# A hybrid decoder layer on eight cores: row statistics by matmul, two queues for the last chunk's copies, and another order of the projection's side work

## What is computed

```python
h = rms_norm(x, norm_mix_g)
z = h @ w_in                       # columns: q 1024 | k 256 | v 256 | u_val 1024 | u_gate 1024
q = rope(rms_norm(q, q_norm_g), pos)
k = rope(rms_norm(k, k_norm_g), pos)
a = attn_prompt(q, k, v, sinks)
u = u_val * jax.nn.sigmoid(u_gate)
c, new_c = causal_dwconv(u, c_buf, conv_w, conv_b)
c = jax.nn.silu(layer_norm(c, conv_ln_g, conv_ln_b))     # over the 1024 channels
x = x + jnp.concatenate([a, c], axis=-1) @ w_out
hm = rms_norm(x, norm_mlp_g)
x = x + jnp.square(jax.nn.relu(hm @ w_up)) @ w_down
```

## Time and profile before

| | us |
|---|---|
| the three times | 1243.03, 1243.94, 1368.0 |
| median shown | 1243.94 |
| profiled execution, its own time | 1243.03 |
| its span on core 4, the slowest | 1241.5 |
| spans of the eight cores | 1235.1 to 1241.5 |
| PE busy | 1191.1 (96%) |
| DVE, ACT, POOL busy | 823.4 (66%), 388.3 (31%), 78.6 (6%) |

### The profile page before, as it was taken

How to read it: one execution, slowest core, us unless ns; L and a number is a source line. 1 busy time by engine, 2 the same in 40 slices (tenths; PEclk the granted TensorE clock), 3 DMA queues, 4 the chain that set the end, 5 groups by cost and what they waited for, 6 DMA issues and landing times.

```text
span 1241.5 us, 26331 instructions; the slowest of 8 cores (1235.1 to 1241.5 us)
## 1 busy us (share of the span) xinstructions
PE 1191.1 (96%) x10375; PEld 943.6 (76%) x10375; DVE 823.4 (66%) x1288; ACT 388.3 (31%) x535; POOL 78.6 (6%) x135
## 2 busy tenths in 40 slices
PE   5859999999989999999999999999999999999998
PEld 3536555555657888888888888888888888888887
DVE  5736866666486967676667676666767666766765
ACT  3536555655144544320004330002332001333000
POOL 2301000000001000000000000000000000000000
PEclk9989999999999999999999999999999999999999
DMA  9995164575949796549966556994444995444795
GB/s 245 217 159 58 20 117 91 106 168 109 241 81 181 199 224 121 90 75 238 241 126 97 90 86 132 259 207 80 92 96 84 250 233 113 95 80 91 178 245 193
DMA packets 56637, 180.27 MB, mean 145 GB/s; under 512 B 20140, under 2 KB 23340, under 8 KB 42540
## 3 DMA queue, kind: packets, MB, share of 16 engines
q0 software_dynamic: 29664, 90.74, 46.5%
q1 hardware_dynamic: 21812, 57.21, 13.8%
q10 hardware_dynamic: 5040, 30.65, 7.4%
HBM read 227.44 MB, written 34.68 MB: 211 GB/s over the span
## 4 chain that ended last, share of the span: by engine, by line
PE 83%; DMA 11%; DVE 3%; ACT 1%; issue 1%; SPq 1%; DVEq 0%; POOL 0%; ACTq 0%; POOLq 0%
PE psum L625 83%; DMA arena<-xt 3%; DVE arena L589 3%; ACT arena L585 1%; DMA x<-arena 1%; DMA arena<-x 1%; DMA arena<-arena 1%; DMA arena<-wdn 1%; DMA arena<-tab 1%; DMA arena<-wup 1%; DMA arena<-wq 1%; SPq L572 1%; DVEq L383 0%; POOL arena L572 0%; ACTq L383 0%
## 5 line engine op out<-in xcount | busy, mean ns | idle before, releaser
L625 PE MATMUL psum<-arena 128*128 128x258 f16 (+10 forms) x10375 | 1191.1, 287 | 47.0 <-DMA arena<-wkv 15.8
L625 PEld LDWEIGHTS psum<-arena 128*128 128x128 bf16 (+3 forms) x10375 | 943.6, 98 | 294.2 <-issue 94.0
L589 DVE TENSOR_TENSOR arena<-arena 128x1024 f16<-128x1024 bf16 (+9 forms) x751 | 504.7, 701 | 198.7 <-ACT arena L585 123.8
L589 DVE TENSOR_TENSOR arena<-psum,arena 128x516 f32<-128x516 f32 (+8 forms) x477 | 329.5, 698 | 202.6 <-PE psum L625 178.3
L585 ACT ACTIVATE arena<-arena 128x512 f32<-128x512 f32 (+10 forms) x266 | 251.6, 959 | 281.8 <-DVE arena L589 231.7
L607 ACT COPY arena<-psum 128x516 f32<-128x516 f32 (+2 forms) x69 | 39.7, 575 | 365.1 <-PE psum L625 353.3
L585 ACT ACTIVATE arena<-psum 128x512 bf16<-128x512 f32 (+8 forms) x140 | 77.0, 579 | 130.3 <-PE psum L625 126.9
L585 ACT ACTIVATE arena<-psum,arena 128x344 f32<-128x344 f32 (+6 forms) x50 | 28.1, 589 | 54.2 <-PE psum L625 50.5
L572 POOL DMA_DIRECT2D arena<-wdn x32 | 17.0, 531 | 386.2 <-PE psum L625 349.0
L572 POOL DMA_DIRECT2D arena<-wup x32 | 17.1, 534 | 374.2 <-PE psum L625 369.0
L602 DVE TENSOR_SCALAR arena<-arena 128x1160 bf16<-128x1160 f32 (+2 forms) x27 | 16.0, 592 | 11.9 <-DMA arena<-xt 10.9
(11 more groups left out here) (10 smaller groups left out, 4.4 us busy)
## 6 DMA issues: line engine op xcount, KB each, us to landing
arena<-wup POOLq DMA_DIRECT2D x32, 1024.0 KB, 9.8
arena<-wdn POOLq DMA_DIRECT2D x32, 1024.0 KB, 12.7
arena<-x ACTq DMA_DIRECT2D x23, 1032.0 KB, 13.2
x<-arena SPq DMA_DIRECT2D x15, 1032.0 KB, 14.8
arena<-xt SPq DMA_DIRECT2D x16, 580.0 KB, 15.7
arena<-arena SPq DMA_DIRECT2D x128, 65.8 KB, 4.9
x<-arena SPq DMA_DIRECT2D x16, 516.0 KB, 10.6
arena<-wu POOLq DMA_DIRECT2D x16, 512.0 KB, 7.5
```

The costliest lines, as they stand in the source:

```text
L589: return P.add(eng, lambda e: e.tensor_tensor(out=out.ap, in0=in0.ap, in1=in1.ap, op=op), reads=[in0, in1], writes=[out], cost=cost(eng, o ...
L625: return P.add("pe", lambda e: e.matmul(out.ap, lhsT.ap, rhs.ap, start=start, stop=stop, skip_group_check=free), reads=[lhsT, rhs], writes ...
```

## The change

Four things change in the stages above.

1. Row statistics per token come from PE: ten float32 matmuls with 128 (last: 4) columns of `SS1` as stationary and one column of ones as moving operand give a column for each V tile in bank 6 (`ptk`), and two `Ln` and two `Exp` make `RTK` of it. The ten DMAs go. The last round's special order goes; only tiles 4 to 7 are copied to `VR`, and tiles 0 to 3, 8 and 9 are scaled straight out of their banks, tiles 0 to 3 ahead of the spreads. Tile 9 gets bank 4.
2. The last chunk's 16 copies alternate between SP and ACT, and the first convolution block of that chunk waits for all of them.
3. The residual loads of tiles 4 to 6 (rows 8 to 10) wait for these copies, those of the next three for the copies and a projection tile; six of the twelve that ACT issued are issued by SP.
4. In the projection both last convolutions come earlier (chunk 6 ahead of all tiles, chunk 7 after two), `ln_stats` after three, the eight `ln_chunk` stand at tiles 6, 7, 8, 10, 11, 12, 13, 14 in place of 7 to 14, and odd tiles up to 13 use banks 3 to 5. The squares of chunk 6 use the buffer of chunk 7.

```diff
@@ -663,7 +663,7 @@
     memset("dve", ONM(), 1.0 / 1024.0)
     KPC = [(0, 512), (512, 1024), (1024, 1156)]
     kps = [ps_f32(2 * i, 2, (2, 512)) for i in range(2)]
-    vps = {t: ps_f32(b, 1, (2, 256)) for t, b in ((0, 4), (1, 4), (2, 5), (3, 5), (4, 6), (5, 6), (6, 7), (7, 7), (8, 7), (9, 7))}
+    vps = {t: ps_f32(b, 1, (2, 256)) for t, b in ((0, 4), (1, 4), (2, 5), (3, 5), (4, 6), (5, 6), (6, 7), (7, 7), (8, 7), (9, 4))}
 
     def v_mm(ti, ps, kc, start, stop):
         tn, c0, nt = TT[ti]
@@ -687,13 +687,10 @@
         if kc >= 2:
             tt("dve", SS1(), SS1(), SQX[(kc - 1) % 2](), ALU.add)
         P.group()
-        late = range(4) if kc == 15 else range(8)
-        for ti in (6, 7, 4, 5) if kc == 15 else ():
-            v_mm(ti, vps[ti], kc, False, ti % 2 == 1)
         for i in range(2):
             for h in range(2):
                 mm(kps[i](h), WKV(kc, (128 * h, 128 * h + 128)), HT(kc, KPC[i]), kc == 0, kc == 15)
-        for ti in late:
+        for ti in range(8):
             v_mm(ti, vps[ti], kc, kc == 0 and ti % 2 == 0, kc == 15 and ti % 2 == 1)
     tt("dve", SS1(), SS1(), SQX[1](), ALU.add)
     cosd = dma("sp", COS(), R(tab_d[:, 0:HW]), "cos", after=[xd[12]])
@@ -714,9 +711,9 @@
     cp("act", I4(), CST((384, 416)))
     act(ESK(), SKT, AF.Exp)
 
-    VR = [sb(O_H + 12288 + 2048 * i, F32, (2, 256)) for i in range(4)]
-    for i in (3, 2, 1, 0):
-        cp("act" if i % 2 else "dve", VR[i](), vps[2 * i]())
+    VR = [sb(O_H + 12288 + 2048 * i, F32, (2, 256)) for i in range(2)]
+    cp("act", VR[1](), vps[6]())
+    cp("dve", VR[0](), vps[4]())
 
     def v_tile(ti):
         P.group()
@@ -724,7 +721,13 @@
             v_mm(ti, vps[ti], kc, kc == 0, kc == 15)
 
     v_tile(8)
-    v_tile(9)
+    P.group()
+    ptk = ps_f32(6, 1, (10,))
+    for ti, (tn, c0, nt) in enumerate(TT):
+        mm(ptk((ti, ti + 1), p=(0, nt)), SS1((c0, c0 + nt)), ONF((0, 1)), True, True)
+    for tr_, pp in (((0, 9), (0, 128)), ((9, 10), (0, SPC))):
+        act(RTK(tr_, p=pp), ptk(tr_, p=pp), AF.Ln, bias=EPS, scale=1.0 / D)
+        act(RTK(tr_, p=pp), RTK(tr_, p=pp), AF.Exp, scale=-0.5)
     RB = sb(O_X, F32, (HW,))
     EB = sb(O_H + 4096, BF16, (HW,))
 
@@ -752,7 +755,7 @@
     SQR = [sb(O_H + 2048 * i, BF16, (2, 512)) for i in range(2)]
     nrope = [0]
 
-    def rope(ps2, n, c0, g, out, out_f32=None, bk=None):
+    def rope(ps2, n, c0, g, out, out_f32=None):
 
         i = nrope[0] % 2
         nrope[0] += 1
@@ -761,7 +764,7 @@
         for h in range(2):
             act(xg(h, nn), ps2(h, nn), AF.Identity, scale=g[h])
         act(sq((0, 2), nn), ps2((0, 2), nn), AF.Square)
-        ss = ps_f32(6 + i if bk is None else bk, 1, (n,))
+        ss = ps_f32(6 + i, 1, (n,))
         P.group()
         mm(ss(), O128(), EB((c0, c0 + n)), True, False)
         mm(ss(), BD(), sq(0, nn), False, False)
@@ -779,21 +782,23 @@
         else:
             tt("dve", out, RA((0, 2), nn), rb, ALU.mult)
 
-    for i in range(3):
-        spread(i, 6 - i)
-    for ti, (tn, c0, nt) in enumerate(TT):
-        dma("sp", RTK((ti, ti + 1), p=(0, nt)), RB((c0, c0 + nt), p=(0, 1)), "rtk", group=True)
+    for ti in range(4):
+        v_out(ti, vps[ti])
+    spread(0, 6)
+    v_tile(9)
+    spread(1, 5)
+    spread(2, 6)
+    for ti in (8, 9):
+        v_out(ti, vps[ti])
     for i in range(2):
-        rope(kps[i], 512, KPC[i][0], GK, KT((0, 2), KPC[i]), bk=6 - 2 * i)
-    kp2 = ps_f32(5, 1, (2, 132))
+        rope(kps[i], 512, KPC[i][0], GK, KT((0, 2), KPC[i]))
+    kp2 = ps_f32(4, 1, (2, 132))
     P.group()
     for h in range(2):
         for kc in range(16):
             mm(kp2(h), WKV(kc, (128 * h, 128 * h + 128)), HT(kc, KPC[2]), kc == 0, kc == 15)
-    for ti in (8, 9):
-        v_out(ti, vps[ti])
-    for ti in range(8):
-        v_out(ti, VR[ti // 2])
+    for ti in range(4, 8):
+        v_out(ti, VR[ti // 2 - 2])
     rope(kp2, 132, 1024, GK, KT((0, 2), KPC[2]), out_f32=KF())
     dma("sp", R(nkt), Ref(KF.ap.rearrange("p a b -> p (a b)"), KF().rngs), "kvout", group=True, final=True)
     dma("sp", R(nvp), VF_L(), "kvout", group=True, final=True)
@@ -876,7 +881,10 @@
             if pi == 2:
                 tt("dve", UF(c), acc((322, 356)), sg((322, 356)), ALU.mult)
 
+    u4_all = []
+
     def u_done(c):
+        u4_all.clear()
         ub, u4 = UB[c % 2], U4[c % 2]
         first = None
         for s in range(4):
@@ -884,9 +892,12 @@
                 src = Ref(ub.ap[32 * g:32 * g + 32, 2 + s:2 + s + UL], ub((0, NU)).rngs)
                 dst = Ref(u4.ap[32 * s:32 * s + 32, g, 0:UL])
                 i = 4 * s + g
-                last = P.add("sp", (lambda src=src, dst=dst: (lambda e: e.dma_start(out=dst.ap, in_=src.ap)))(),
+                last = P.add("act" if c == 7 and g % 2 else "sp", (lambda src=src, dst=dst: (lambda e: e.dma_start(out=dst.ap, in_=src.ap)))(),
                       reads=[src], writes=[u4()] if i == 0 else [], claim=[u4()] if i == 15 else [],
-                      key="u4%d" % (c % 2), cost=600, nbytes=65800)
+                      key="u4%d%s" % (c % 2, "a" if c == 7 and g % 2 else ""), cost=600, nbytes=65800,
+                      after=first.deps if c == 7 and i == 1 else ())
+                first = first or last
+                u4_all.append(last)
         cw4 = PAR((312 + 32 * c, 344 + 32 * c))
         tt("dve", D4[c % 2](), Ref(I4().ap.unsqueeze(1).unsqueeze(1).broadcast_to([128, 4, 8, 32]), I4().rngs),
            Ref(cw4.ap.rearrange("p (g t) -> p g t", t=8).unsqueeze(3).broadcast_to([128, 4, 8, 32]), cw4.rngs), ALU.mult)
@@ -901,14 +912,17 @@
     def conv_job(c, pi):
         acc = dense_bank(512)
         P.group()
+        n = len(P.streams["pe"])
         for t in range(8):
             for g in range(4):
                 mm(acc(p=(32 * g, 32 * g + 32)), D4[c % 2](g, t),
                    U4[c % 2](g, (4 * t + 512 * pi, 4 * t + 512 * pi + 512)), t == 0, t == 7)
+        if c == 7:
+            P.streams["pe"][n].deps.update(u4_all)
         act(CC(c, (512 * pi, 512 * pi + 512)), acc(), AF.Identity, bias=CB(c))
 
     def conv_sums(c, eng="dve"):
-        sq = SQT if c < 7 else SQT7
+        sq = SQT if c < 6 else SQT7
         act(sq(), CC(c), AF.Square)
         if c == 0:
             cp(eng, S1(), CC(c))
@@ -1018,7 +1032,7 @@
 
     XT = sb(O_A, F32, (16, NM))
     def xt_load(dc):
-        dma("sp" if dc < 4 else "act", XT(dc), R(xt_d[dc][:, MC0:MC0 + NM]), "xt%d" % dc, after=gate_xt)
+        dma("sp" if dc < 4 or 8 <= dc < 14 else "act", XT(dc), R(xt_d[dc][:, MC0:MC0 + NM]), "xt%d" % dc, after=gate_xt)
 
     for dc in range(4):
         xt_load(dc)
@@ -1062,9 +1076,6 @@
         tt("dve", CC(c), CC(c), RSL(), ALU.mult)
         act(CT(c), CC(c), AF.Silu, bias=LB(c), scale=LG(c))
 
-    conv_job(6, 0)
-    conv_job(6, 1)
-    conv_sums(6)
     xt_next = [4]
 
     def xt_more(n):
@@ -1073,29 +1084,36 @@
                 xt_load(DCO[xt_next[0]])
                 xt_next[0] += 1
 
+    gate_xt = list(u4_all)
+    xt_more(3)
     gate_xt = []
-    xt_more(3)
 
     def wo_first(i):
         nonlocal gate_xt
-        wo_half(DCO[i], 0, AT, 0 if i % 2 == 0 else 3 if i < 7 else 4)
-        gate_xt = [P.streams["pe"][-1]]
+        wo_half(DCO[i], 0, AT, 0 if i % 2 == 0 else 3 if i < 15 else 4)
+        gate_xt = [P.streams["pe"][-1]] + (u4_all if i < 3 else [])
         xt_more(1)
 
-    for i in range(3):
+    for i in range(0):
+        wo_first(i)
+    conv_job(6, 0)
+    conv_job(6, 1)
+    conv_sums(6)
+    for i in range(0, 2):
         wo_first(i)
     conv_job(7, 0)
     conv_job(7, 1)
     conv_sums(7)
-    for i in range(3, 5):
+    for i in range(2, 3):
         wo_first(i)
     ln_stats()
-    for i in range(5, 16):
+    lnw = {6: [0], 7: [1], 8: [2], 10: [3], 11: [4], 12: [5], 13: [6], 14: [7]}
+    for i in range(3, 16):
         wo_first(i)
         for bk in {14: (0, 2), 15: (4, 6)}.get(i, ()):
             memset("dve", Buf("ps", psum[:, bk, :], 2048 * bk, (512,), 4)((256, SEG)), 0.0)
-        if 7 <= i < 15:
-            ln_chunk(i - 7)
+        for c in lnw.get(i, ()):
+            ln_chunk(c)
 
     O_HM = O_B + 64
     HM = sb(O_HM, F16, (8, 7, HT2))
```

## The result

| | before | after |
|---|---|---|
| executions counted, us | 1243.03, 1243.94 | 1226.8, 1227.01, 1227.15 |
| profiled execution, us | 1243.03 | 1227.15 |
| its span, slowest core | 1241.5, core 4 | 1225.6, core 7 |
| PE busy | 1191.1 | 1191.8 |

The ratio is 0.9867, with a 95% interval of 0.9839 to 0.9896: 16.5 us less, and by the interval 13 to 20. PE's work is the same; what went is idle time.

What follows compares the result with a forecast made beforehand. PE was taken as the bound, busy 1191.1 of 1241.5 us, so only its idle and low-clock time could go. 11.05 + 3.9 = 14.95 off 1243.03 gave 1228.1, forecast as 1229, range 1224 to 1236.

Steps and rivals of the forecast that it cites:

- Part one: Row statistics on PE in place of ten copies: 11.05 us gained after costs, bounds 7.4 and 12.65.
- the 15.25: Row statistics, gain before costs in us: PE's stall 12.64, faster matmuls behind it 1.58, two following gaps 1.03.
- Cost (a): Last round: tile 8 waits for ACT's copy out of its bank, costing PE 0.8 us (0.6 to 1.5).
- Cost (b): Row statistics: ten one-column float32 matmuls with twenty stationary loads cost PE 2.9 us, between 2.0 and 3.8.
- Cost (c): New order of ACT and PE: ACT reaches banks only just ahead of PE, costing 0.5 us (0 to 1.5).
- Part two: Last chunk's convolution and projection: 6.52 us of gaps less a new 2.6 wait, 3.9 gained, bounds 6.5 and -2.1.
- the LayerNorm's new places: Projection: at most two LayerNorm operations between two DVE additions, so PE's 6.52 us of idle time goes.
- Copies in time: Rival, 15 in 100: last chunk's convolution finds its rows landed and row-statistics costs are low; 1224.8 us.
- The engines, not the issue: Rival, 10 in 100: engines set the copies' landing, PE waits 10.8 us before the last convolution; 1238.9 us.
- Masks take RTK's place: Rival, 8 in 100: ACT waits for constant tables from SP's queue after the row statistics, losing 5 us; 1234 us.
- The wait stays: Rival, 4 in 100: PE's row-statistics stall has another cause, such as query weights; a later part alone gives 1240 us.
- Gated rows late: Rival, 3 in 100: gated residual rows delay the fifth projection tile's addition and its banks; over 1244 us.

Runs made afterwards that it cites:

- b_only: Kernel before with only the second part changed (last chunk's copies, convolution order, gated residual rows, LayerNorm rows, banks), row statistics still by ten copies; ratio 0.9969, 3.9 us less.
- hold_wo: Changed kernel with one 512 KB load of output weights asked for only when all sixteen copies have landed; ratio to the kernel before 0.9839, 1222.56 us.
- ln_banks: Changed kernel with LayerNorm rows listed at tiles 7 to 14 and accumulators from tile 7 on in banks 4 to 6, as before; ratio to the kernel before 0.9877.
- masks_late: Kernel before with SP issuing the loads of par and cst behind the ten row copies instead of ahead of them; ratio 0.9971.
- conv_later: Changed kernel with the last chunk's convolution behind four output tiles instead of two, LayerNorm statistics behind the fifth; ratio to the kernel before 0.9831.
- one_queue: Changed kernel with all sixteen copies issued by SP; the planner also moved the last convolution behind five tiles instead of two; ratio to the kernel before 0.9884.
- wq_held: Kernel before with the second half of the query weights (eight loads) asked for only when the ten row copies have landed; ratio 0.9894.
- a_only: Kernel before with only the row statistics changed, ten one-column matmuls in place of ten copies; ratio 0.9895, 13.1 us less.

## Why the prediction was right, and where it was wrong

**The time.** 1229 was said, with a range of 1224 to 1236; 1227.1 came. The size and the two places of the gain were right, the closeness of the number partly luck: core 4, for which the sum was made, gained 22.9 (6.8 of them in the MLP), core 7, now the slowest, 9.5. The first step that failed is in how the numbers follow from the sum, the sentence that 2% is about what a measurement of this kernel can tell from no change. Two executions before stood at 1243.03 and 1243.94, and the interval of the ratio is 0.3% wide on either side. A forecast of 1.2% was therefore a forecast of faster, not of no change, and should have been called so; only the part over 2% was rightly put at 3 in 100.

**Part one, 11.05 said.** Core 4 gained 94.88 - 82.57 = 12.3, so the costs were 2.9 of the 15.25, not 4.2. That the other cores gain as much or more fails for cores 1 and 5 (10.9 and 9.5), whose wait before had been the shortest. Cost (a), 0.8, came as 0.82. Cost (b), 2.9, was 2.3: the ten one-column matmuls are twenty records, here on core 7 with their loads:

```profile
L625 PE MATMUL psum<-arena 128*128 128x1 f32 x18 | 2.1, 246 | 0.0
L625 PE MATMUL psum<-arena 128*4 128x1 f32 x2 | 0.2, 165 | 0.0
L625 PEld LDWEIGHTS psum<-arena 128*128 128x128 f32 x24 | 3.1, 191 | 0.6 <-issue 0.2
```

The float32 load of 128 columns takes 191 ns here (24 of them: eighteen of these and the spreads' six), near the 189 of the earlier trace rows, but twenty times that, 3.8, was not paid: PE shows 2.3 and no gap. The Trainium skill (TensorE: Matmul & The Clock Gate, LDWEIGHTS) gave by its rule an estimate of 107 ns a load and 2.1 for the whole; the trace contradicts it for a load, with 191, and comes near it in the sum, with 2.3. Cost (c), 0.5, was nothing: PE has no other gap up to 125. The clock of 86.2 to 99.3, 0.90 before, is 1.00 on core 4. A cost that the sum does not have stands on core 5, the clock behind the one-column matmuls, 1.7 us. It is no accident of that core: in the profiled executions of the ten kernels that have these matmuls the clock falls to 0.50 within 1.3 us of their end on 27 of the 80 cores; in the four kernels without them it falls between 53 and 63 us on none of the 32.

**Part two, 3.9 said.** `b_only` gave 3.9, core 4 gained 301.69 - 297.87 = 3.8. Yet the way there was a mean of unlike cores. The step of the mechanism that failed is the copies' landing: I took 4.9, the median of all 128, and a wait of 2.6. The median landing was 5.5 to 7.3, the wait 1.9 to 3.0 on four cores and 3.9 to 5.1 on four, because a load of 512 KB of output weights, which I named only against a rival and left out of the sum, starts beside the copies (2.1 to 2.3 and no wait with it held, `hold_wo`); and I left the clock to the bounds. On core 7 the 0.50 of 310 to 315 loses 2.5 us of the 6.5, the wait 5.1, and the stretch came out 1.6 longer than before. What I gave to the LayerNorm's new places does not depend on them (`ln_banks`). Two of the signs fail on some cores: the clock of 1.00 between 50 and 140 (core 5), and behind conv 7 DVE ends gaps of 0.51 to 1.28 on cores 1, 2, 5 and 7, all near 432, ahead of the MLP.

**Core 4 stays the longest.** It does not. Its lead was 5.25 us of MLP gaps in the one execution that was profiled. In `masks_late`, whose MLP is untouched, such gaps sum to 8.29 on core 7 and 0.67 on core 4. The waits of core 7 there, from 455 us on (total, times, longest), show what they go with:

```profile
DVE arena L589 <- DMA arena<-wdn: 32.0, 16, 5.0
DVE arena L589 <- DMA arena<-wup: 21.5, 9, 5.6
PE psum L625 <- DVE arena L589: 8.3, 17, 1.8
```

Core 4 waits 21.5 and 11.5 for the same loads, and its PE 0.7.

**The rivals.** *Copies in time* (1224.8): not in the changed kernel, but `hold_wo` and `conv_later` are that case. *The engines, not the issue* (10 in 100): half right, and 10 in 100 was too little. The copies land in 2.2 us without the weights and 6.9 beside them; yet with one queue the wait grows by 4. The Trainium skill (DMA: Bandwidth & Descriptors, Issuing engines are not separate DMA queues) says that more issuers save only issue time, usually small beside the transfer. The trace agrees on the shared engines; here sixteen issues took 11.2 us and a copy beside the weights 6.9, so it was not small. *Masks take RTK's place*: no; ACT copies them at 78.9 without waiting for a DMA:

```profile
78.31 0.69 ACT L585 ACTIVATE arena<-arena 128x8 f32<-128x8 f32 x2
78.90 0.80 ACT L607 CAST arena<-arena 128x128 bf16<-128x128 f32 x4
```

*The wait stays*: no, but the query weights named there were behind it, one step further back, as what made the copies slow. *Gated rows late*: not in the changed kernel; in `one_queue` it happened as described, 8.55 us on PE.

## What to carry to other kernels

When a tiny transfer takes long, look for the loads that share its time before replacing it: holding eight loads that were not yet needed (`wq_held`) gave what ten matmuls and a new order gave, with a far smaller edit. Ask of a new wait not only how long it is at the median but what other transfer starts beside it on each core, and put a few more microseconds of ready work ahead of it: two tiles more (`conv_later`) took the wait away on every core. Where a planner orders the code, an edit to a queue or a gate can move the very thing that it was meant to test, so read the order before the result.

## What the runs showed of the hardware

- The last of ten copies of at most 512 bytes took 16.2 and 15.0 us beside sixteen loads of query weights, 3.5 to 4.3 when eight of these were held. Copies of 65.8 KB took at the median 2.1 to 2.3 with the output weights held, 5.5 to 7.3 beside one load of 512 KB.
- The clock after a wait is not a matter of the wait's length alone. In the changed kernel core 0 waited 1.87 and core 3 waited 3.02, with 1.00 behind; core 4 waited 2.16 and ran at 0.50 from 306 to 308; core 7 after 5.13 from 310 to 315. In `a_only` the same 72 matmuls after a gap of 2.06 to 2.07 took 10.62 on cores 0 and 4 and 12.30 on core 1 (mean clock 0.86).
- The clock can fall while PE is busy all the time: behind twenty records of float32 matmuls with one moving column, on 27 of 80 cores, as on core 5 of the changed kernel (0.52 from 57 to 60 us, 1.7 us lost). What makes it fall on some cores and not on others stays open.
- Of the cores 0 and 1, 2 and 3, 4 and 5, 6 and 7 one is longer than its neighbour in every profiled execution shown here, by 2.4 to 8.6 us, and not always the same one. Over 103 counted executions of the kernels here, the two of such a pair differ by less than 2 us in 3 of 412 cases; cores paired otherwise (0 and 2, 1 and 3, 4 and 6, 5 and 7) do so in 171. In the changed kernel it is the one that waits longer before conv 7. What the two share was not tried and stays open.
